# A decoder layer with routed experts: the first gate spread over the partitions by products with ones, and the last projection's blocks issued in another order

## The reference

```python
mod = silu(c) @ w_ada + b_ada                 # 6144 numbers, one vector for all tokens
shift1, scale1, gate1, shift2, scale2, gate2 = split(mod, 6)
h  = rms_norm(x) * (1 + scale1) + shift1
x  = x + gate1 * mixer(h)                     # conv branch and attention branch, gated, then @ w_o
h2 = rms_norm(x) * (1 + scale2) + shift2
x  = x + gate2 * moe(h2)                      # top 4 of 32 experts, w_up 1024x2048, w_down 1024x1024 each
```

## Time and profile before

| | us |
|---|---|
| median of 3 runs | 1279.64 |
| lowest, highest | 1279.39, 1280.59 |
| the profiled execution | 1280.47 |
| its span | 1278.7 |

### The profile page before, as it was taken

One profiled execution on the slowest core, in us unless ns is written; L12 is line 12 of the kernel. 1 busy time (PEld: TensorE's weight loads), 2 busy tenths in 40 slices (PEclk: granted clock), 3 DMA queues, 4 the chain that ended last, 5 costly groups with the idle time before them and its releaser, 6 DMA issues.

```text
span 1278.7 us, 23403 instructions
## 1 busy us (share of the span) xinstructions
PE 1067.0 (83%) x9826; PEld 523.0 (41%) x9826; DVE 418.8 (33%) x1150; ACT 244.3 (19%) x646; POOL 43.6 (3%) x74
## 2 busy tenths in 40 slices
PE   8999999998499556569999567978769696999995
PEld 5864488885143121123434122423224242444432
DVE  1499975735242111112222111312112121323221
ACT  1135344700131000001211000201001020112210
POOL 2000000304200000000000000000000000000000
PEclk9999999998799988889999888998879798999997
DMA  9995532889779999999999999999999999799997
GB/s 328 337 322 180 176 141 93 297 335 368 295 284 427 426 428 427 428 427 427 426 428 427 427 427 428 427 427 428 427 427 426 427 428 426 321 412 428 426 428 312
DMA packets 66493, 475.81 MB, mean 372 GB/s; under 512 B 6417, under 2 KB 20182, under 8 KB 39670
## 3 DMA queue, kind: packets, MB, share of 16 engines
q1 hardware_dynamic: 62676, 472.54, 90.0%
q10 hardware_dynamic: 3746, 2.21, 0.6%
HBM read 473.03 MB, written 1.05 MB: 371 GB/s over the span
## 4 chain that ended last, share of the span: by engine, by line
PE 45%; DMA 31%; SPq 15%; issue 5%; ACT 2%; DVE 1%; ACTq 1%; another core or an unknown queue 0%; DVEq 0%
DMA weights<-in_w_down 25%; SPq L471 15%; PE bank L1657 13%; PE bank L1687 7%; PE bank L1369 6%; PE bank L1376 5%; DMA weights<-in_w_up 4%; PE bank L1305 2%; PE bank L1361 2%; PE bank L1598 2%; PE bank L1585 1%; DMA u_conv<-weights 1%; PE bank L1605 1%; DMA weights<-in_w_ada 1%; PE bank L1522 1%
## 5 line engine op out<-in xcount | busy, mean ns | idle before, releaser
L1657 PE MATMUL bank<-weights,buf_d 128*32 128x512 f32 x3008 | 390.1, 664 | 137.1 <-DMA weights<-in_w_up 137.1
L1657 PEld LDWEIGHTS bank<-weights,buf_d 128*32 128x32 f32 x3008 | 95.7, 116 | 396.9 <-DMA weights<-in_w_up 203.8
L1687 PE MATMUL bank<-weights,buf_d 128*32 128x256 f32 x3008 | 178.2, 383 | 40.9 <-DMA weights<-in_w_down 38.0
L1254 DVE TENSOR_SCALAR u_conv<-bank 128x256 f32<-128x256 f32 x47 | 20.0, 425 | 458.1 <-PE bank L1657 458.1
L828 ACT ACTIVATE u_conv<-u_conv 128x256 f32<-128x256 f32 x47 | 19.6, 417 | 697.3 <-DVE u_conv L1254 697.3
L1687 PEld LDWEIGHTS bank<-weights,buf_d 128*32 128x32 f32 x3008 | 90.9, 110 | 114.5 <-DMA weights<-in_w_down 49.4
L933 DVE SCALAR_TENSOR_TENSOR weights<-u_conv,weights 128x256 f32<-128x256 f32 x240 | 96.9, 477 | 0.4
L1369 PE MATMUL bank<-weights,buf_d 128*128 128x512 f32 x192 | 82.6, 592 | 0.0
L1266 DVE TENSOR_TENSOR buf_d<-bank,u_conv 128x256 f32<-128x256 f32 x47 | 20.0, 425 | 178.9 <-PE bank L1687 178.9
L828 ACT ACT_TABLE_LOAD x47 | 60.3, 1283 | 1.4 <-issue 0.6
L1376 PE MATMUL bank<-buf_d,weights 128*128 128x256 f32 x256 | 58.2, 380 | 0.0
(11 more groups left out here) (275 smaller groups left out, 825.9 us busy)
## 6 DMA issues: line engine op xcount, KB each, us to landing
weights<-in_w_up SPq DMA_DIRECT2D x128, 2048.0 KB, 39.0
weights<-in_w_down SPq DMA_DIRECT2D x63, 2048.0 KB, 44.1
weights<-in_w_in SPq DMA_DIRECT2D x10, 2048.0 KB, 15.3
weights<-in_w_ada SPq DMA_DIRECT2D x8, 2048.0 KB, 7.9
weights<-in_w_ada SPq DMA_DIRECT2D x8, 1024.0 KB, 11.3
weights<-in_w_in SPq DMA_DIRECT2D x8, 512.0 KB, 9.0
weights<-in_w_in SPq DMA_DIRECT2D x4, 1024.0 KB, 13.9
weights<-in_w_conv_out SPq DMA_DIRECT2D x2, 2048.0 KB, 8.4
```

The lines of the kernel that those rows point to most:

```text
L1657: ins = t.matmul(UP[SLOTS * g:SLOTS * g + SLOTS, :], xgT[:, r, SLOTS * j:SLOTS * j + SLOTS], up_group(w[:, r, :], g), start=False, stop=(j ...
L1687: ins = t.matmul(DOWN[rows, 0:T], actT[:, r, at:at + SLOTS], w[:, g, r, T * q:T * q + T], start=False, stop=(h == 1 and g == 1 and r == 1))
```

## The change

gate1 no longer goes through transfers. After w_o 0, TensorE multiplies a 128x128 matrix of ones with each half of the summed gate part, into two banks that the attention scores used (`spread_gates`), so that each partition gets the sum. ScalarE copies the two banks into `gate1`. The bias of the gate is added on one partition before the sum, by two small VectorE instructions among the `mod_product`s (`add_gate_bias`). `sum_rows(0)` keeps only its last two groups. The rows and their transposes use fixed banks 6 and 7 and are no longer in `order`. Four small transfers for gate2 remain, after set 1 alone. In SyncE's queue chunk (0,1) goes before the last ADA block, and WO0 goes before the waits of chunk (0,2). GpSimd's bias work waits for set 1 instead of set 0.

```diff
-        order += [("y_conv", i) for i in (1, 2)] + [("ada", 1)]
-        order += [("oT", i) for i in range(4)] + [("y_conv", 3), ("mod2T", 1)]
+        order += [("y_conv", i) for i in (1, 2)]
+        order += [("oT", i) for i in range(4)] + [("y_conv", 3)]
         order += [("y_attn", i) for i in range(4)]
-        order += [("w_o", 0), ("w_o", 1), ("ada", 0), ("w_o", 2), ("mod2T", 0), ("w_o", 3)]
+        order += [("w_o", i) for i in range(4)]
...
-                if n == WO0:
+                if n == ADA0[0] + 3:
                     full(sp, OT_USE + 3)
                     load_chunk(0, 1)
+                if n == WO0 + 1:
                     sp.wait_ge(*used[ADA0[0]])
                     load_chunk(0, 2)
-                if n == WO0 + 1:
                     sp.wait_ge(*used[ADA0[0] + 1])
                     load_chunk(0, 3)
                 sp.wait_ge(*used[n - RING])
...
-            sp.wait_ge(mod_ready, 16 * 12)
+            sp.wait_ge(mod_ready, 16 * 4)
...
-            pool.wait_ge(mod_summed[0], KD)
+            pool.wait_ge(mod_summed[1], KD)
...
-            for gi in range(2):
-                act_e.wait_ge(bank_free[ADA_USE[gi] % 4], ADA_USE[gi] // 4 + 1)
+            act_e.wait_ge(rows_kept[1], 1)
             for i in range(2):
-                for q in range(4):
-                    load(gate1[32 * q:32 * q + 32, NB * i:NB * i + NB], modrow2[32 * i:32 * i + 32, 0, :], mod_ready)
                 for q in range(2):
                     load(gate2[64 * i + 32 * q:64 * i + 32 * q + 32, :],
                          modrow2[64 + 32 * i:96 + 32 * i, 1, T * q:T * q + T], mod_ready)
+            for i in range(2):
+                act_e.wait_ge(gate_rows, i + 1)
+                s.copy(gate1[:, NB * i:NB * i + NB], PS[4 + i][:, :]).then_inc(gate_kept, 1)
...
+            def add_gate_bias(k, i):
+                part, at = slice(32 * i, 32 * i + 1), slice(NB * i, NB * i + NB)
+                w = blk(ADA0[0] + k // 2, 2)[:, k % 2, :]
+                dve.wait_ge(in_rows2, 128)
+                dve.wait_ge(mod_summed[0], k + 1)
+                step(v.tensor_tensor(w[part, at], w[part, at], modrow2[part, 0, :], ALU.add))
...
                 for k in (2 * i, 2 * i + 1):
                     mod_product(0, k)
+                if i in (1, 2):
+                    add_gate_bias(2 * i + 1, i - 1)
             ada_row(0)
-            dve.wait_ge(mod_ready, 16 * 12)
             def add_branch(tt, half):
-                use = WO_USE[2 * tt + half]
+                use = WO_USE + 2 * tt + half
                 full(dve, use)
+                dve.wait_ge(gate_kept, half + 1)
...
+            dve.wait_ge(mod_ready, 16 * 4)
             count = dve.value_load(unit_ends[0:1, EXPERTS - 1:EXPERTS], min_val=EXPERTS, max_val=UCOLS - 1)
...
+            def spread_gates():
+                pe.wait_ge(mod_summed[0], KD)
+                total = blk(ADA0[0] + 3, 2)[:, 1, :]
+                for i in range(2):
+                    t.matmul(PS[4 + i][:, :], ones[:], total[:, NB * i:NB * i + NB], start=True, stop=True).then_inc(gate_rows, 1)
+                sum_rows(0, (2, 3)).then_inc(rows_full[0], 1)
...
                 ins.then_inc(bank_full[use % 4], 1)
+                if i == 0:
+                    spread_gates()
                 if i == 1:
-                    sum_rows(0)
-                if i == 2:
+                    pe.wait_ge(cols_kept[1], 1)
                     turn_rows(0)
...
+            pe.wait_ge(gate_kept, 2)
             seed(0)
```

More of the change, by code:

```diff
@@ L275, in build @@
         mod_summed = [sem(f"mod_summed{gi}") for gi in range(2)]
+        gate_rows, gate_kept = sem("gate_rows"), sem("gate_kept")
+        rows_full, rows_kept, rows_turned, cols_kept = (
+            [sem(f"{n}{gi}") for gi in range(2)] for n in ("rows_full", "rows_kept", "rows_turned", "cols_kept"))
         pick_ready, pickw_ready, sel_ready, gathered, xs_ready, xt_done, xm_ready, cmb_ready = (
@@ L383, in build @@
         YA_USE = use_of["y_attn", 0]
-        WO_USE = [use_of["w_o", i] for i in range(4)]
-        M2T_USE = [use_of["mod2T", i] for i in range(2)]
+        WO_USE = use_of["w_o", 0]
         X1T_USE = [use_of["x1T", i] for i in range(4)]
@@ L410, in build @@
             used_by(CONV0 + i, CONV_USE + 2 * i + 1)
+        for gi in range(2):
+            used[ADA0[gi] + 3] = (rows_full[gi], 1)
         for i in range(4):
@@ L414, in build @@
         for i in range(2):
-            used_by(ADA0[i] + 3, ADA_USE[i])
             used_by(V0 + i, V_USE[2 * i + 1])
@@ L418, in build @@
             used_by(AOUT0 + i, YA_USE + 2 * i + 1)
-            used_by(WO0 + i, WO_USE[2 + i])
+            used_by(WO0 + i, WO_USE + 2 + i)
         def bank(use):
@@ L511, in _ @@
             load_chunk(1, 2)
-            sp.wait_ge(mod_ready, 16 * 12)
+            sp.wait_ge(mod_ready, 16 * 4)
             for gi in range(2):
-                full(sp, M2T_USE[gi])
+                sp.wait_ge(rows_turned[gi], 1)
             sp.wait_ge(ebias_ready, 3 * PARTS)
@@ L785, in _ @@
                          modrow2[64 + 32 * i:96 + 32 * i, 1, T * q:T * q + T], mod_ready)
+            for i in range(2):
+                act_e.wait_ge(gate_rows, i + 1)
+                s.copy(gate1[:, NB * i:NB * i + NB], PS[4 + i][:, :]).then_inc(gate_kept, 1)
             def square(tt, half):
-                freed(act_e, WO_USE[2 * tt + half])
+                freed(act_e, WO_USE + 2 * tt + half)
                 if tt or half:
@@ L889, in ada_row @@
             def ada_row(gi):
-                use = ADA_USE[gi]
                 dve.wait_ge(in_rows2, 128)
-                full(dve, use)
-                v.tensor_tensor(modrow2[:, gi, :], bank(use)[:, :], modrow2[:, gi, :], ALU.add).then_inc(bank_free[use % 4], 1)
+                dve.wait_ge(rows_full[gi], 1)
+                part = slice(0 if gi else 64, P)
+                v.tensor_tensor(modrow2[part, gi, :], PS[6][part, :], modrow2[part, gi, :], ALU.add).then_inc(rows_kept[gi], 1)
+            def add_gate_bias(k, i):
[4 more added lines that the diff above has]
+                step(v.tensor_tensor(w[part, at], w[part, at], modrow2[part, 0, :], ALU.add))
             def mod_product(gi, k):
@@ L1013, in _, with columns @@
             conv(3, 2, TAPS)
-            def columns(gi, first):
-                return bank(M2T_USE[gi])[:, :].rearrange("p (h r q z) -> p q h r z", h=2, r=2, q=4)[:, first:first + 2, :, :, 0]
+            def columns(first):
+                return PS[7][:, :].rearrange("p (h r q z) -> p q h r z", h=2, r=2, q=4)[:, first:first + 2, :, :, 0]
             by_chunk = mod2[:, :, :].rearrange("p m (i h r) -> p m i h r", i=2, h=2)
@@ L1102, in _ @@
             mix_conv(3)
-            full(dve, M2T_USE[1])
-            v.scalar_tensor_tensor(by_chunk[:, 1, :, :, :], columns(1, 0), 1.0, gain, ALU.add, ALU.mult).then_inc(
-                bank_free[M2T_USE[1] % 4], 1)
+            dve.wait_ge(rows_turned[1], 1)
+            v.scalar_tensor_tensor(by_chunk[:, 1, :, :, :], columns(0), 1.0, gain, ALU.add, ALU.mult).then_inc(cols_kept[1], 1)
             dve.wait_ge(gate_ready, 2)
@@ L1129, in _ @@
             add_branch(0, 1)
-            full(dve, M2T_USE[0])
-            v.tensor_copy(by_chunk[:, 0, :, :, :], columns(0, 2)).then_inc(bank_free[M2T_USE[0] % 4], 1)
+            dve.wait_ge(rows_turned[0], 1)
+            v.tensor_copy(by_chunk[:, 0, :, :, :], columns(2)).then_inc(cols_kept[0], 1)
             dve.wait_ge(in_moe, 16)
@@ L1392, in turn_rows, with sum_rows @@
             def turn_rows(gi):
-                use = M2T_USE[gi]
-                fill(pe, use)
-                freed(pe, ADA_USE[gi])
+                pe.wait_ge(rows_kept[gi], 1)
                 for h in range(2):
                     for r in range(2):
-                        ins = t.transpose(bank(use)[:, P * (2 * h + r):P * (2 * h + r) + P],
+                        ins = t.transpose(PS[7][:, P * (2 * h + r):P * (2 * h + r) + P],
                                           modrow2[:, gi, T * h:T * h + T].rearrange("p (c r) -> p r c", r=2)[:, r, :], ident[:])
[L1400 to L1405, removed]
+                ins.then_inc(rows_turned[gi], 1)
+            def sum_rows(gi, groups):
                 total = blk(ADA0[gi] + 3, 2)[:, 1, :]
-                for q in range(4):
-                    ins = t.matmul(bank(use)[32 * q:32 * q + 32, :], ones[:, 0:32], total[:, NB * q:NB * q + NB],
+                for q in groups:
+                    ins = t.matmul(PS[6][32 * q:32 * q + 32, :], ones[:, 0:32], total[:, NB * q:NB * q + NB],
                                    start=True, stop=True)
-                ins.then_inc(bank_full[use % 4], 1)
+                return ins
+            def spread_gates():
[4 more added lines that the diff above has]
+                sum_rows(0, (2, 3)).then_inc(rows_full[0], 1)
             for i in range(8):
@@ L1493, in _ @@
                 conv_out(i)
-            sum_rows(1)
```

(4 more changed lines are left out.)

3 lines of the change are left out of this document (1 added, 2 removed).

## The result

| | before | after |
|---|---|---|
| median, us | 1279.52 | 1257.51 |
| lowest, highest | 1279.31, 1280.59 | 1256.88, 1257.89 |
| the profiled execution, its span | 1280.47, 1278.7 | 1257.4, 1255.7 |

The ratio is 0.9826, with a 95% interval of 0.9809 to 0.9843. That is 22.0 us by the medians and 23.0 us by the spans; the profiled execution of before was itself 0.95 us above its median. (The medians are now of four runs each; the prediction started from 1279.64, the median of three.) The forecast was 1256.2, in a range of 1254 to 1262.

The account below looks back on a forecast made before the run. The expert-weight stream was taken to end the kernel, so its start, set by w_o 3's end, had to move. Earlier w_o loads, full clock and gate spreading without loads summed to 23.4 us: 1279.64 to 1256.2, range 1254 to 1262.

Parts of the forecast that it names:

- The date to follow: End of w_o 3, which precedes the last add_branch and the expert stage: 331.5 instead of 354.94, 23.4 us gained.
- rival 3: Expert stage: its end hangs on something that does not move with its start, so no gain, 1279.6; 2%.
- The two pauses and w_o 0: TensorE at w_o 0: the 3.22 us pause goes, full clock makes the block 7.11 us instead of 9.97.
- rival 1: Before and in w_o 0: pause not WO0's and stays, 1262.3, or only the clock falls, 1259.1; together 8%.
- WO1: Second w_o load, needed by w_o 1: lands 3.7 us earlier, at 309.3, just before TensorE needs it at 309.5.
- their issue times leave no hole: Stream up to WO1: each block is issued before the one ahead has landed, so WO1 lands at 309.3.
- Spreading: TensorE behind w_o 0: products with ones 1.8 us plus sum_rows(0)'s two groups 1.0, together 2.8, to 309.5.
- The stream's margin: Chunk stream near 343: the DMA engines are just not the limit, with 1.8 us to spare.
- Rival 2: Chunks after WO1: DMA engines become the bound at 361 GB/s, 4.5 us lost, 1260.7; 7%.
- The sign: Whole kernel: faster 96%, same 2%, slower 2%, with about 2.6 us needed to tell from no change.
- Rival 4: Between w_o 0 and w_o 1: TensorE held by spread_gates waiting for the late last ADA block, slower, 1285; 2%.
- The median: Whole kernel: median of the runs before, 1279.64, minus 23.4 gives 1256.2.

Follow-up runs that it names:

- e1: The changed kernel with SyncE's old queue order (WO0 behind chunk (0,2), chunk (0,1) behind the last ADA block): 1260.81 us, ratio 0.9861.
- e5: The changed kernel with chunk (0,3) issued right behind WO1 instead of ahead of it: 1258.08 us, ratio 0.9833.
- e3: The changed kernel with gate1 spread by eight 64 KB loads as before and no products with ones: 1262.59 us, ratio 0.9865.
- e6: Run e3 with the sum over partitions (spread_gates) moved from behind w_o 0 to behind w_o 1: 1268.54 us, ratio 0.9911.
- e2: The kernel before with the new order of SyncE's queue alone: 1276.50 us, ratio 0.9971.
- e9: The changed kernel with VectorE's products 0 to 2 moved before y_attn, others spread over its blocks, chunk (0,2) issued ahead of WO0: 1255.56 us, ratio 0.9806.
- e4: The changed kernel with GpSimd's bias work waiting for the sums of set 0 again, as before: 1257.35 us, ratio 0.9824.
- e7: Run e6 with one wait more, w_o 3 waiting until add_branch(0,1) has freed its bank: 1270.63 us, ratio 0.9937.

## Why the prediction was right

- **The date to follow.** The gain is the date of the last add_branch: 23.06 us there, 23.05 at the first unit, 23.0 at the span's end; forecast 23.4. That an expert stage begun earlier ends earlier by as much (against rival 3) is shown by the 910 us above.
- **The two pauses and w_o 0.** As forecast: WO0 issued at 286.16 landed after 7.7 us; w_o 0 started with no pause, at full clock, and took 7.03. e1 shows that the pause was WO0's (against rival 1's first half). The 2.9 us of clock are right for the trace of before, but no fixed price: e1 had 1.5 behind such a pause.
- **WO1.** This is the term of TensorE's sum that was missed. Forecast to land at 309.3, just in time, it landed at 310.5, and w_o 1 waited 1.07 us for it. Of these 1.2 us, 0.37 is not the change's: the trace after stands about 0.4 us late at 207 us already. The other 0.8 is the step "their issue times leave no hole". The prediction took it that a chunk issued before the one ahead has landed keeps the stream full. Chunk (0,3) was issued at 296.8, 2.0 before (0,2) landed, and the stream still sank (row below), which at 428 GB/s is 0.8 us lost; in e5, where nothing was queued behind (0,2), nothing moved from 298 on, 0.8 before its landing. By luck, part came back: I took 7.1 us a block, but the blocks follow each other more closely (6.87 us from start to start of w_o 0 and the spreading). From w_o 1's start to w_o 3's end it took 21.3 us and not 22.0, so w_o 3 ended 0.4 late, at 331.9, and not 1.1.

```profile
298.00:300.00 2.00, 2.00 (x11) 1.74 (x10) 1.89 (x2) 0.00 (x0) 0.00 (x0) 1.00 0.89 254
```

- **Spreading.** 1.88 and 1.05, one into the other, 2.86 from start to end; forecast 2.8. The bias on one partition took 0.68, the upper bound, as if it had 128 partitions, and was hidden as forecast: VectorE's products ended at 306.1 instead of 305.7, 0.5 us ahead of the spreading (forecast 1.0).
- **The stream's margin.** The forecast had the engines "just not the limit". They show one hole, 213 GB/s from 344 to 346, 1 us of stream. e5 shows that the limit is there as described. Rival 2's condition, a rate of 361 GB/s beside the last chunks, did not come: it was 433.
- **The sign.** Rival 4 did not come: TensorE did not wait for the sum. But the reading against it was off. "Nothing moves from 285 on" does not mean landed by 285: the last ADA block, issued at 271.9, landed 15.6 us later, at 287.5. That left 13.9 us to the products that need it, at 301.4, where the forecast saw 16.
- **The median.** 1256.2 against 1257.51. The rows moved by 23.05 and not 23.4: 0.35. The rest, 0.9, lies in taking the gain from one execution and the start from a median: the profiled execution of before stood 0.83 above the 1279.64 from which the sum started, and that of after 0.11 below its own median. The difference of the medians, 22.0, is the smaller figure.

What the prediction did not say is how the 22 us hang together. It named the landing of the loads as the last link in the chain of waits, and TensorE stood still for 16.5 us behind it. The runs show that loads with the same early start as the products (e3) cost 5. The larger part was their late start behind w_o 1 (5.9, e6 to e3), the queue's order (3.3) and the 8.0 us between e2 and e6, which are not split further. None of it changed the forecast, since the change does all parts at once.

## What to carry to other kernels

A long wait at the end of a chain is not the price of the thing waited for: put the old thing at the new place (e3) before crediting the new thing. Small transfers among 2 MB blocks took 6 to 16 us from issue to landing in these traces, so look at what is queued when the last of them is issued before giving them a price. Where one engine's path and the transfer stream are within 1 to 2 us of each other, a reorder that helps one alone gives nothing (e5), and one that helps both does (e9).

## What the runs showed of the hardware

**GpSimd beside VectorE.** In e9 VectorE's three products beside GpSimd's bias work took 4.10, 2.94 and 4.20 us instead of 2.35, and two of GpSimd's casts 6.03 instead of 2.12 (times on GpSimd are rough). First e9's VectorE line over its seven products, then GpSimd's row in e9 and the same in the changed kernel:

```profile
L911 DVE SCALAR_TENSOR_TENSOR weights<-weights x7: 2343/2352/4203, 274.0 to 297.9; 128x2048 f32<-128x2048 f32 x7
```

```profile
276.03 6.03 POOL L593 CAST late<-weights 32x1024 bf16<-32x1024 f32 x2
```

```profile
275.38 2.12 POOL L592 CAST late<-weights 32x1024 bf16<-32x1024 f32 x2
```

In e4 a 128x256 product of VectorE (L1147) took 2.38 us beside GpSimd instead of 0.42; the GpSimd instruction beside it ran from 319.12 to 321.24, and VectorE's ended 0.3 us behind it:

```profile
319.14 2.38 DVE L1147 TENSOR_TENSOR weights<-weights 128x256 f32<-128x256 f32 x1 [0.23 <-DVE weights L1140]
```

The Trainium skill (GPSIMD Engine Reference, "1. Specifications") says that GpSimd shares its interfaces to SBUF with VectorE and contends with VectorE's instructions that have two inputs in SBUF; both kinds above have two, and the traces agree. That section gives no size; here such an instruction took 0.6 to 2.0 us longer.

**The clock.** After a pause ahead of a block of 16 products, the block ran at half clock at first and took longer than its 7.03 us, but not by the length of the pause: 9.97 (before, pause of 3.2), 8.52 (e1, 3.1), 9.82 (e2, 3.9), 8.64 (e6, 3.8) and 8.80 us (e3, 2.6). In e6 the granted clock stayed at 0.50 from 342 to 354, in the router, after pauses of 2.5 and 2.0 us, although TensorE is shown busy for 7.98 of the 8 us from 344 on. In e3, after pauses of 0.68 and 1.95 at the same place, it was half for 3 us only. In e7, with the long block in front, the router had the full clock. What tells these apart the runs leave open.
